# Decoder layer with 32 experts on one core: residual rows kept once, the gather matrix scaled by their root, and a tenth weight chunk in the running sum's space

## What is computed

```python
h = x + mixer_block(rmsnorm(h, norm_mix))          # Mamba2 scan, short convolution, gates, w_out
h = h + cross_attn(rmsnorm(h, norm_xattn), mem)    # 4 heads, 256 memory tokens
h = h + moe(rmsnorm(h, norm_moe))                  # top 4 of 32 experts
y = rmsnorm(h) * norm_final

def expert_ffn(xb, w_gu, b_gu, w_dn, b_dn):
    gate, up = split(xb @ w_gu + b_gu)             # 1024 -> 2 x 1024
    gate, up = minimum(gate, 7), clip(up, -7, 7)
    return ((up + 1) * gate * sigmoid(1.702 * gate)) @ w_dn + b_dn
```

## Time and profile before

| | |
|---|---|
| median of 3 runs | 1424.09 us (1422.95 to 1424.12) |
| the profiled execution | 1423.08 us |
| its span | 1421.1 us |
| PE busy | 1384.3 us (97%) |
| DVE busy | 447.7 us (32%) |
| ACT busy | 219.2 us (15%) |
| POOL busy | 28.1 us (2%) |
| read from HBM | 486.12 MB |
| granted clock of PE, mean | 0.996 |
| chain that ended last | PE 81%, DMA 15%, DVE 2% |

### The profile page before, as it was taken

How to read it: one execution, slowest core, us unless ns; L and a number is a source line. 1 busy time by engine, 2 the same in 40 slices (tenths; PEclk the granted TensorE clock), 3 DMA queues, 4 the chain that set the end, 5 groups by cost and what they waited for, 6 DMA issues and landing times.

```text
span 1421.1 us, 16026 instructions
## 1 busy us (share of the span) xinstructions
PE 1384.3 (97%) x6385; PEld 681.5 (48%) x6385; DVE 447.7 (32%) x906; ACT 219.2 (15%) x406; POOL 28.1 (2%) x48
## 2 busy tenths in 40 slices
PE   8999999999999999999999999999999999999997
PEld 6788887677756633333333333333233332333322
DVE  5634344862471421211321312213112121121213
ACT  2220022051123400101101001011010110100102
POOL 0000002200000000000000000000000000000000
PEclk9999999999999999999999999999999999999999
DMA  7643435975379599999999999999999999999995
GB/s 253 203 158 129 148 119 176 349 274 223 119 268 406 218 411 387 429 428 428 428 428 428 428 428 428 429 428 428 428 429 428 429 428 428 429 428 428 428 427 231
DMA packets 69782, 494.73 MB, mean 348 GB/s; under 512 B 8443, under 2 KB 9875, under 8 KB 45149
## 3 DMA queue, kind: packets, MB, share of 16 engines
q1 hardware_dynamic: 64652, 477.55, 81.6%
q0 software_dynamic: 4368, 15.53, 3.0%
q10 hardware_dynamic: 724, 1.11, 0.2%
HBM read 486.12 MB, written 8.22 MB: 348 GB/s over the span
## 4 chain that ended last, share of the span: by engine, by line
PE 81%; DMA 15%; DVE 2%; issue 1%; ACT 1%; ACTq 0%; SPq 0%; DVEq 0%
PE bank L1460 77%; DMA flat<-in_w_gate_up 6%; DMA ring<-in_w_gate_up 6%; PE bank L1471 4%; DMA tokT<-in_w_down 2%; DVE wide L1387 1%; DMA ring<-in_w_in 1%; ACTq L608 0%; ACT wide L605 0%; DVE wide L1392 0%; ACT wide L596 0%; PE bank L1917 0%; DVE wide L1443 0%; ACT L615 0%; ACT L645 0%
## 5 line engine op out<-in xcount | busy, mean ns | idle before, releaser
L1460 PE MATMUL bank<-ring,wide 128*64 128x512 f32 (+2 forms) x1696 | 405.3, 595 | 7.3 <-DMA ring<-in_w_gate_up 6.7
L1460 PE MATMUL bank<-wide 128*64 128x512 f32 (+5 forms) x908 | 272.1, 570 | 11.0 <-DVE wide L1387 7.2
L1460 PE MATMUL bank<-tokT,ring 128*128 128x264 f32 x1152 | 266.0, 389 | 2.2 <-DMA ring<-in_w_in 2.2
L1460 PEld LDWEIGHTS bank<-ring,wide 128*64 128x64 f32 (+2 forms) x1696 | 132.5, 140 | 255.8 <-issue 240.1
L1460 PEld LDWEIGHTS bank<-tokT,ring 128*128 128x128 f32 x1152 | 217.3, 191 | 44.1 <-issue 5.4
L1460 PEld LDWEIGHTS bank<-wide 128*64 128x64 f32 (+3 forms) x908 | 92.3, 155 | 170.2 <-issue 116.4
L596 ACT ACTIVATE wide<-bank 64x512 f32<-64x512 f32 (+3 forms) x105 | 58.8, 561 | 334.5 <-PE bank L1460 212.5
L1411 DVE TENSOR_SCALAR wide<-bank 128x512 f32<-128x512 f32 x32 | 22.1, 692 | 271.3 <-PE bank L1460 271.3
L1460 PE MATMUL bank<-flat,wide 128*64 128x512 f32 (+2 forms) x408 | 92.3, 589 | 3.7 <-DMA flat<-in_w_gate_up 3.7
L1460 PE MATMUL bank<-conv,wide 128*64 128x512 f32 (+1 forms) x400 | 91.1, 596 | 0.3 <-ACT wide L596 0.3
L865 ACT ACTIVATE wide<-wide 128x512 f32<-128x512 f32 x32 | 20.2, 630 | 448.0 <-DVE wide L1411 448.0
(11 more groups left out here) (259 smaller groups left out, 749.3 us busy)
## 6 DMA issues: line engine op xcount, KB each, us to landing
ring<-in_w_gate_up SPq DMA_DIRECT2D x64, 2048.0 KB, 27.1
ring<-in_w_down SPq DMA_DIRECT2D x32, 2048.0 KB, 28.4
flat<-in_w_gate_up SPq DMA_DIRECT2D x16, 2048.0 KB, 27.3
conv<-in_w_gate_up SPq DMA_DIRECT2D x16, 2048.0 KB, 26.3
tokT<-in_w_gate_up SPq DMA_DIRECT2D x16, 2048.0 KB, 27.7
wide<-in_w_gate_up SPq DMA_DIRECT2D x16, 2048.0 KB, 26.8
ring<-in_w_in SPq DMA_DIRECT2D x15, 2048.0 KB, 11.8
wide<-in_w_down SPq DMA_DIRECT2D x8, 2048.0 KB, 25.5
```

The costliest lines, as they stand in the source:

```text
L1460: last[0] = pe.matmul(out, lhsT, rhs, start=start, stop=stop)
```

## The change

Four things are changed together.

- `xtok` holds the raw rows, written once, straight from PSUM by `raw_tokens`. The second copies (times `rr`) are gone. `select` becomes two instructions: the comparison, and a product with `rr` broadcast over the 128 slots, so that `gather` gives normalized rows. For that `rr` of the sample rows is also written to partitions 32 to 39, by one more ACT root.
- `acc` is no longer filled ahead of the experts. In the first pair `accumulate` writes `acc` = bank + `xtok` (`fresh`).
- The first pair's scatter reads the biases straight from `bdn` and the gates from `gT`, 32 rows each. ScalarE's two copies into `ytok` and POOL's two memsets are gone.
- The first 4096 columns of the region (`before_acc`, where `acc` and `ytok` will be) are slot 9, which takes chunk 5 of the first pair, once. `AHEAD` is 10. It is asked for after slot 0 and once the values are stored (`v_out`).

```diff
+        before_acc = moe[:, 0:4 * D]
...
-        FIRST_SLOT = [0, 1, 2, 6, 3, 4, 5, 7, 8, 0, 1, 2]
-        AHEAD = 9
+        FIRST_SLOT = [0, 1, 2, 6, 3, 9, 4, 5, 7, 8, 0, 1]
+        AHEAD = 10
...
-            for j, name, k in ((2, "so", 1), (4, "so", 1), (5, "so", 3), (0, "so", 3), (1, "xo", 3), (3, "xo", 7)):
+            for j, name, k in ((2, "so", 1), (4, "so", 1), (5, "so", 3), (0, "so", 3), (9, "so", 3), (1, "xo", 3), (3, "xo", 7)):
                 filled(sp, name, k)
+                if j == 9:
+                    sp.wait_ge(S["v_out"], 16)
                 first_chunk(FIRST_SLOT.index(j))
...
-            for g, done_stages in zip(range(AHEAD, AHEAD + 8), (1, 2, 3, 5, 6, 7, 8, 9)):
+            for g, done_stages in zip(range(AHEAD, AHEAD + 8), (1, 2, 3, 5, 7, 8, 9, 10)):
                 sp.wait_ge(S["stage_done"], done_stages)
                 refill(g, g // 12)
...
-                for g in range(17, 41):
+                for g in range(18, 42):
                     sp.wait_ge(S["stage_done"], it * 24 + (g - 7))
...
-            pool.memset(ytok, 0.0).then_inc(S["scr_zero"], 1)
-            pool.memset(gT, 0.0).then_inc(S["scr_zero"], 1)
...
-                    move("xtok", 3 * h + t, acc[0:n, t, 512 * h:512 * h + 512], 512, n)
+                    move("xtok", 3 * h + t, xtok[t][0:n, 512 * h:512 * h + 512], 512, n)
...
-            done(s.activation(rr[0:TS, 2:3], b[0:TS, 2:3], ACT.Sqrt, bias=eps[0:TS, 0:1], scale=1.0 / D), "rs")
+            s.activation(rr[0:TS, 2:3], b[0:TS, 2:3], ACT.Sqrt, bias=eps[0:TS, 0:1], scale=1.0 / D)
+            done(s.activation(rr[32:32 + TS, 2:3], b[0:TS, 2:3], ACT.Sqrt, bias=eps[0:TS, 0:1], scale=1.0 / D), "rs")
             raw_tokens(1)
-            emptied(s, "xtok", 4)
-            s.wait_ge(S["v_out"], 16)
-            s.wait_ge(S["rr_ready"], 1)
-            done(copy(xtok[32:32 + TS, 2, 0:512], filled(s, "xtok", 5)[0:TS, 0:512], rr[0:TS, 2:3]), "xtok", 5)
-            copy(xtok[0:TS, 2, 0:512], acc[0:TS, 2, 0:512], rr[0:TS, 2:3]).then_inc(S["xtok_ready"], 1)
-            for t, n in TILES_P:
-                copy(xtok[0:n, t, :], acc[0:n, t, :], rr[0:n, t:t + 1]).then_inc(S["xtok_ready"], 1)
...
-            s.wait_ge(S["scr_zero"], 2)
-            for h in range(2):
-                copy(ytok[0:E, 512 * h:512 * h + 512], bdn[:, 512 * h:512 * h + 512]).then_inc(S["ytok_ready"], 1)
...
             def select(e0):
 
-                ranked(selT, e0).then_inc(S["sel_ready"], 1)
+                st(ranked(selT, e0))
+                v.tensor_tensor(out=selT, in0=selT, in1=bc(rr[:, 0:3], P), op=ALU.mult).then_inc(S["sel_ready"], 1)
...
-                return v.tensor_tensor(out=dst, in0=bank[6 + j % 2][:, :], in1=dst, op=ALU.add)\
-                    .then_inc(S["scat_read"], 1)
+                return v.tensor_tensor(out=dst, in0=bank[6 + j % 2][:, :], op=ALU.add,
+                                       in1=xtok[t][:, 512 * h:512 * h + 512] if fresh else dst).then_inc(S["scat_read"], 1)
...
-            pe.wait_ge(S["xtok_ready"], 3)
...
-                mm(bank[6 + j % 2][:, :], gT[:, t * P:t * P + P], ytok[:, 512 * h:512 * h + 512])
+                    mm(bank[6 + j % 2][:, :], gT[0:k, t * P:t * P + P], rows[0:k, 512 * h:512 * h + 512])
...
-            experts(first_pair, 0)
+            experts(first_pair, 0, bias_rows=True)
```

More of the change, by code:

```diff
@@ L252, in build @@
         xg = cut(KB * P).rearrange("p (k n) -> p k n", k=KB)
+        gT = cut(T)
+        at[0] = SCC * T
+        xtok += [cut(D)]
         mrows, srows = moe[0:11, at[0]:at[0] + 2048], moe[0:10, at[0] + 2048:at[0] + 3072]
@@ L280, in build @@
         slot_full = [sem(f"slot_full{i}") for i in range(6)]
-        moe_full = [sem(f"moe_full{i}") for i in range(9)]
+        moe_full = [sem(f"moe_full{i}") for i in range(10)]
         x_in = [sem(f"x_in{t}") for t in range(3)]
@@ L813, in raw_tokens @@
                 for t, n in TILES_P:
-                    move("xtok", 3 * h + t, acc[0:n, t, 512 * h:512 * h + 512], 512, n)
+                    move("xtok", 3 * h + t, xtok[t][0:n, 512 * h:512 * h + 512], 512, n)
                 if h == 0:
-                    move("xtok", 2, acc[0:TS, 2, 0:512], 512, TS)
+                    move("xtok", 2, xtok[2][0:TS, 0:512], 512, TS)
                 else:
-                    copy(acc[32:32 + TS, 2, 0:512], filled(s, "xtok", 5)[0:TS, 0:512])
+                    done(copy(xtok[2][32:32 + TS, 0:512], filled(s, "xtok", 5)[0:TS, 0:512]), "xtok", 5)
             for k in range(KB):
@@ L825, in _ @@
                 if k == 4:
+                    s.wait_ge(S["v_out"], 16)
                     raw_tokens(0)
@@ L897, in _ @@
                 s.wait_ge(S["tile_done"], i + 1)
-                st(s.activation(xtok[0:n, t, :], acc[0:n, t, :], ACT.Square, accum_out=rfin[0:n, t:t + 1]))
+                st(s.activation(xtok[t][0:n, :], acc[0:n, t, :], ACT.Square, accum_out=rfin[0:n, t:t + 1]))
                 s.activation(rfin[0:n, t:t + 1], rfin[0:n, t:t + 1], ACT.Sqrt, bias=eps[0:n, 0:1], scale=1.0 / D)\
@@ L1377, in _, with accumulate @@
             n = v.value_load(npass[0:1, 0:1], min_val=0, max_val=MAXP - 1)
-            v.wait_ge(S["xtok_ready"], 3)
+            emptied(v, "xtok", 5)
             n0, order = st.n, [None, (0, 0), (0, 1), (1, 0), (1, 1)]
-            def accumulate(at, j, last=False):
+            def accumulate(at, j, last=False, fresh=False):
                 v.wait_ge(S["scat_full"], at(5, j + 1))
@@ L1387, in accumulate @@
                         ins = v.tensor_tensor(out=acc[0:TS, 2, 512 * h:512 * h + 512] if last else acc[rows, 2, 0:512],
-                                              in0=bank[6][rows, :], in1=acc[rows, 2, 0:512], op=ALU.add)
+                                              in0=bank[6][rows, :], op=ALU.add,
+                                              in1=xtok[2][rows, 0:512] if fresh else acc[rows, 2, 0:512])
                     return ins.then_inc(S["scat_read"], 1)
@@ L1391, in accumulate, with experts @@
                 dst = acc[:, t, 512 * h:512 * h + 512]
-                return v.tensor_tensor(out=dst, in0=bank[6 + j % 2][:, :], in1=dst, op=ALU.add)\
-                    .then_inc(S["scat_read"], 1)
-            def experts(at, pair, after, final=False):
+                return v.tensor_tensor(out=dst, in0=bank[6 + j % 2][:, :], op=ALU.add,
+                                       in1=xtok[t][:, 512 * h:512 * h + 512] if fresh else dst).then_inc(S["scat_read"], 1)
+            def experts(at, pair, after, final=False, fresh=False):
                 if not final:
@@ L1959, in gather @@
                     rows = slice(32 * h, 32 * h + TS)
-                    mm(bank[4 + h][:, :], selT[rows, 2, :], xtok[rows, 2, 0:512], True, False)
+                    mm(bank[4 + h][:, :], selT[rows, 2, :], xtok[2][rows, 0:512], True, False)
                 for h in range(2):
                     for t in range(2):
-                        mm(bank[4 + h][:, :], selT[:, t, :], xtok[:, t, 512 * h:512 * h + 512], False, t == 1)
+                        mm(bank[4 + h][:, :], selT[:, t, :], xtok[t][:, 512 * h:512 * h + 512], False, t == 1)
                     last[0].then_inc(S["xy_full"], 1)
@@ L1973, in turn_rows, with scatter @@
                     last[0].then_inc(S["xgt_turned"], 1)
-            def scatter(at):
-                pe.wait_ge(S["ytok_ready"], at(4, 2))
+            def scatter(at, k=P, rows=ytok):
+                if rows is ytok:
+                    pe.wait_ge(S["ytok_ready"], at(4, 0))
                 pe.wait_ge(S["gT_ready"], at(1, 1))
                 for h in range(2):
-                    mm(bank[6][32 * h:32 * h + TS, :], gT[:, TP:T], ytok[:, 512 * h:512 * h + 512])
+                    mm(bank[6][32 * h:32 * h + TS, :], gT[0:k, TP:T], rows[0:k, 512 * h:512 * h + 512])
                 last[0].then_inc(S["scat_full"], 1)
@@ L1998, in _, with experts @@
             n = pe.value_load(npass[0:1, 0:1], min_val=0, max_val=MAXP - 1)
-            def experts(at, pair, it=None, final=False):
+            def experts(at, pair, it=None, final=False, bias_rows=False):
                 def landed(j):
@@ L2055, in experts @@
                 turn_acts(0)
-                scatter(at)
+                if bias_rows:
+                    scatter(at, E, bdn)
+                else:
+                    scatter(at)
                 gate_up(1, 2)
```

39 lines of the change are left out of this document (19 added, 20 removed).

## The result

The changed kernel takes **1427.96 us** (median of 7 runs, 1426.97 to 1430.14). The kernel before, run beside it, takes 1424.09 (7 runs, 1422.84 to 1426.26). The ratio is 1.0032, with a 95% interval of 1.0021 to 1.0042: slower by 3.9 us, which is more than the 0.2% that the prediction named as what can be told from no change. The forecast was 1424.8, with a range up to 1426.3. The profiled execution took 1428.22 us, with a span of 1426.3.

A forecast was written before the change was run, and what follows sets the result against it. DMA was taken to set the end from stage 9 of the first pair on. Root 0.16 plus product 0.59, all else 0, gave +0.75 on 1423.08; with 1.01 to the median, 1424.8 us, range 1422.9 to 1426.3.

The forecast's parts named there:

- The frame: Whole experts part: stage 9 of the first pair starts DMA's unbroken stream, 176 chunks of 4.91 us, and fixes the end.
- The tenth chunk, 0: Start of the experts: the extra chunk fills a DMA hole but is paid back as rest before stage 7; 0 us.
- Rival A: DMA stream: the tenth chunk is worth its transfer, 4.9 us, giving 1419.9 or 1416.9 us; chance 0.07.
- Root +0.16: Router chain ahead of the experts: one more ACT root delays VectorE's reciprocal by 0.16 us, bounds 0 and 0.24.
- product +0.59: First `select`: the product with `rr` delays PE's first gather by 0.59 us in full, bounds 0.47 and 0.81.
- Removed from ACT, 0 on the path: Ahead of the experts: dropped scaled copies are off the path; slot 6's chunk up to 3 us sooner ends in DMA's rest.
- The first scatter with 32 rows, 0 with bounds -0.5 and 0: First pair's scatter: ten products of the same 512 columns take the same time, as columns set PE's pace; 0 us.
- rival B: Between warming products and first gate-up: PE's added rest drops the clock to 1.2 GHz, some 5 us, 1429.9 us; chance 0.05.

The follow-up runs named there:

- no_tenth: full_rows without the tenth slot, with nine chunks ahead and the old lists of slots and waits; 1424.99 us.
- full_rows: The changed kernel with the first scatter over 128 rows again, 96 of them zero; 1424.64 us, ratio 1.0004.
- before_32: The kernel before with only the first pair's scatter cut to 32 rows; 1426.9 us, ratio 1.0028.
- no_root: The changed kernel without the product with `rr` in `select`, so the experts read rows not normalized; 1427.32 us, ratio 1.0027.
- bias_mid: bias_last with the bias scatter in the 14th pair instead of the last, pairs 14 and 15 written out; 1419.51 us, ratio 0.9972.
- bias_last: full_rows with the bias scatter moved from the first pair to the last, and chunk 9 in slot 9; 1420.5 us, ratio 0.9976.
- full_rows_again: full_rows once more, unchanged, on another chip; 1425.44 us, ratio 1.0009.
- warm4: full_rows with one more call of warming products ahead of the first gather; 1425.15 us, ratio 1.0008.
- rows_64: full_rows with 64 rows in the first scatter, half of them zeros; 1426.6 us, ratio 1.0017.
- bias_last_slot5: bias_last with chunk 5 in slot 9 and the changed kernel's refill waits; 1421.94 us, ratio 0.9986.
- bias_mid_warm4: bias_mid with one more call of warming products ahead of the first gather; 1420.22 us, ratio 0.9974.

## Why the prediction was wrong

**The frame was right.** DMA sets the end from stage 9 of the first pair on. Stage 9 came 4.91 us later in the profiled executions, and the last chunk 5.19.

**The tenth chunk, 0: right.** DMA is busy in 466 to 467 (377 GB/s, where it moved nothing before), there is no refill behind stage 6, and DMA rests instead in 520 to 529. no_tenth measures the chunk at nothing that can be told. Rival A fell.

**Root +0.16 and product +0.59: mechanism right, sizes near.** They measured 0.28 and 0.60. The root was under-sized because the third one starts 0.24 after the second (477.79, 478.03), not 0.16, and the bound of 0.24 was just missed. Together 0.87 instead of 0.75. full_rows, which has both and holds the clock behind the scatter, is at 1.0004 and in its repeat 1.0009, that is +0.6 and +1.3 us, with medians of 1424.64 and 1425.44 on either side of the forecast of 1424.8. This agreement is in part luck: if only runs with a mean clock of 0.998 or more are taken on both sides, full_rows is 1.45 us over the kernel before and its repeat 1.56 (3 to 15 runs a side). The traces account for 0.87 of that; the rest stays open.

**Removed from ACT, 0 on the path: right.** The issue of slot 6's chunk came at 491.58 instead of 493.12, 2.25 us sooner when the offset of 0.71 is taken off. It ended in DMA's rest, as said.

**The first scatter with 32 rows, 0 with bounds -0.5 and 0: this step failed.** It was costed by the duration of a product, and that part was true: at full clock six instructions with 32 rows take 2.08 us, and in full_rows six with 128 rows take 2.09. (So the cheaper weight loads of the lower bound are not seen either, and the ten products that the prediction counts are twelve instructions.) What was not costed is what such products do to the clock. It fell for some 7 us, and the term that stood at 0 measured 3.15 (before_32) to 3.33 us (changed kernel) of PE's time, right in front of stage 9, where nothing covers it. The row that was used for a bound, 16 products with 32 rows in 1.95 us, runs four row groups side by side, so it is no single narrow product and could not show this. The upper bound of 0 was the fault: the text names the clock as a risk for the rest ahead of the gather, prices it there (rival B, +5 us, chance 0.05), and does not ask the same of the edit that gives PE fewer rows. B had the right effect, a fall, with another cause and at another place: 484 to 492 shows 1.00 in the changed kernel's profile, and no_root shows that neither the gather's lateness nor the rest in front of it matters for the fall behind the scatter.

The sum of what was measured: 0.87 for root and product, 3.15 (before_32) to 3.33 (changed kernel) for the 32 rows, about 4.0 to 4.2 in all, against 3.87 between the medians. The profiled executions differ by 5.14 (1428.22 and 1423.08): the one of before was 1.01 us under its own median, the one of the changed kernel 0.26 over.

The Trainium skill, TensorE: Matmul & The Clock Gate, section Why this matters for your kernels, ties a drop of the clock in mid-kernel to PE standing idle between bursts of matmuls. Here it fell with PE shown as busy from 493.22 on but for 0.43 us, so the measurement goes further than the page. The same section says that a single product with 32 rows takes as long as one with 128; the trace agrees at full clock (2.08 and 2.09 us for six), and by that sentence alone the change would cost nothing.

## What to carry to other kernels

An edit that gave PE's products fewer rows (a shorter contraction) saved no time here and cost the clock of the stretch behind them; padding with zero rows held it. So the clock behind an edit of this kind has to be costed too. Read the granted clock in stretches of 1 us, since neither the busy share nor the profile's 40 slices show a fall of 7 us, and read the mean clock of every run beside its time. Where DMA sets the end, find the last rest of DMA and what ends it. Here a chunk loaded ahead of that point was worth nothing that can be told, while work taken from PE's path in front of it moved the end as far: in bias_mid stage 9 came 4.77 us sooner than in full_rows and the last products 5.14. Work that is moved has to land where PE waits anyway; in the last pair it made PE the one that ends last.

## What the runs showed of the hardware that was not expected

**The number of rows made the difference, zeros or not.** The scatter's products with 32 rows brought the clock to 0.50 in all three profiles that have them (the changed kernel, before_32, no_root), and no run of these kernels has a mean clock above 0.996. The same products over 128 rows with 96 rows of zeros held 1.00 in every profile that has them, and those over 64 rows did so in the one profile there is. What happens between 32 and 64 rows was not tried, and why the rows matter stays open. A few narrow products among wide ones did no harm: the changed kernel's gather at 532 has four instructions with 8 rows ahead of eight with 128, and the clock stays at 1.00 in it and behind it.

**Falls in some executions of one program.** Between 478 and 492 us, a stretch of small products with waits, six profiled executions show a clock of 0.50 for some microseconds (at about 480: bias_last, full_rows_again, warm4; from just ahead of the gather on: rows_64, bias_last_slot5, bias_mid_warm4), and the profiles of before, the changed kernel, before_32, full_rows, no_tenth, no_root and bias_mid show none. full_rows and full_rows_again are the same program. Here are two stretches of bias_last:

```profile
478.00:479.00 1.00, 0.88 (x7) 0.47 (x5) 0.93 (x7) 0.98 (x3) 0.00 (x0) 0.72 1.00 426
479.00:480.00 1.00, 1.00 (x7) 0.64 (x6) 0.92 (x5) 0.98 (x3) 0.00 (x0) 0.50 0.90 377
```

The first 22 us of the span show falls of the same kind in nine of the thirteen profiled executions, those of before and of the changed kernel among them, and none in full_rows, before_32, rows_64 and bias_mid_warm4. The first root starts at 476.64 to 477.07 us in the first three of these, and at 476.91 (before), 477.62 (changed kernel) and 477.85 (full_rows_again) where there was such a fall. All this is part of the spread of 2 to 7 us that the runs of one kernel show; what decides it stays open. A small step in a median, such as the 0.0011 of no_tenth, is therefore not read as an effect of its edit.
